# A block kernel on one core: five sums of squares and sums, from fp32 operands to split fp32r ones

## The reference, cut to what matters

```python
def rms_norm(x, g):
    y = x * rsqrt(mean(x * x, -1) + EPS)
    return y * g
...
# gated linear attention, 4 heads of 128: a norm over the 128 features of each head
o = o * rsqrt(mean(o * o, -1) + EPS)
...
# conformer_conv, 512 channels: a depthwise convolution of width 31, then a layer norm over the channels
y = conv(a * sigmoid(g)) + dw_b
mu = mean(y, -1)
xc = y - mu
y = silu(xc * rsqrt(mean(xc * xc, -1) + EPS) * ln_g + ln_b)
...
# the norm ahead of the feed forward part
hn = rms_norm(h, norm2_g)
h = h + square(relu(hn @ w_ff1)) @ w_ff2
```

## Time and profile before

| what | us |
|---|---|
| median of 3 runs | 878.4 (877.93 to 878.43) |
| the profiled execution | 878.33 |
| its span | 877.0 |
| TensorE busy with matmuls | 867.4 |
| VectorE busy | 725.4 |
| ScalarE busy | 573.4 |

### The profile page before, as it was taken

The page is one execution under the profiler, slowest core; times in us unless marked ns, Lnnn a source line. Parts: engine busy times, 40 slices in busy tenths (PEclk is TensorE's granted clock), DMA queues, the critical chain, the costliest instruction groups (busy, mean ns, idle before and its releaser), DMA issues.

```text
span 877.0 us, 18438 instructions
## 1 busy us (share of the span) xinstructions
PE 867.4 (99%) x7308; PEld 846.6 (97%) x7308; DVE 725.4 (83%) x1168; ACT 573.4 (65%) x851; POOL 2.2 (0%) x10
## 2 busy tenths in 40 slices
PE   9999999999999999999999999999999999999996
PEld 7999989999999999999999999899999999999996
DVE  6788999899988899888887999989788985555554
ACT  7858466675696787664446879677786664444542
POOL 0000000000000000000000000000000000000000
PEclk9999999999999999999999999999999999999999
DMA  8866456566775789989895566754455566666551
GB/s 316 284 197 225 149 164 194 170 191 211 271 243 191 257 290 332 324 299 339 328 336 180 168 220 209 209 166 141 152 166 176 187 201 200 192 194 195 182 161 49
DMA packets 59045, 189.87 MB, mean 216 GB/s; under 512 B 8640, under 2 KB 11088, under 8 KB 58832
## 3 DMA queue, kind: packets, MB, share of 16 engines
q1 hardware_dynamic: 58816, 188.69, 65.0%
q10 hardware_dynamic: 144, 0.00, 0.0%
HBM read 186.57 MB, written 1.05 MB: 214 GB/s over the span
## 4 chain that ended last, share of the span: by engine, by line
PE 91%; ACT 4%; DVE 3%; issue 1%; DMA 1%; SPq 0%; DVEq 0%; ACTq 0%
PE bank L1101 28%; PE bank L1103 27%; PE bank L1104 27%; PE bank L1074 1%; PE bank L1073 1%; PE bank L1072 1%; ACT whi L2048 1%; DMA H<-in_xT 1%; PE bank L1035 0%; DVE wlo L1146 0%; PE bank L1042 0%; PE bank L1038 0%; PE bank L887 0%; PE bank L769 0%; ACT L2252 0%
## 5 line engine op out<-in xcount | busy, mean ns | idle before, releaser
L1146 DVE TENSOR_TENSOR wlo<-raw,whi 128x1024 fp32r<-128x1024 f32 x291 | 353.7, 1221 | 83.2 <-ACT whi L2048 82.6
L2048 ACT ACTIVATE whi<-raw 128x1024 fp32r<-128x1024 f32 x291 | 304.7, 1056 | 169.0 <-PE bank L1104 164.2
L1101 PE MATMUL bank<-Alo,whi 128*128 128x256 f32 x1328 | 371.5, 280 | 0.0
L1103 PE MATMUL bank<-Ahi,wlo 128*128 128x256 f32 x1328 | 367.7, 277 | 0.0
L1104 PE MATMUL bank<-Ahi,whi 128*128 128x256 f32 x1328 | 367.7, 277 | 0.0
L1101 PEld LDWEIGHTS bank<-Alo,whi 128*128 128x128 f32 x1328 | 249.9, 188 | 2.8 <-issue 2.2
L1103 PEld LDWEIGHTS bank<-Ahi,wlo 128*128 128x128 f32 x1328 | 249.5, 188 | 0.4 <-issue 0.2
L1104 PEld LDWEIGHTS bank<-Ahi,whi 128*128 128x128 f32 x1328 | 249.5, 188 | 0.0
L1103 PE MATMUL bank<-Fhi,wlo 128*128 128x256 f32 (+1 forms) x320 | 88.9, 278 | 0.0
L1104 PE MATMUL bank<-Fhi,whi 128*128 128x256 f32 (+1 forms) x320 | 88.9, 278 | 0.0
L1101 PE MATMUL bank<-Flo,whi 128*128 128x256 f32 x256 | 70.8, 277 | 0.0
(11 more groups left out here) (447 smaller groups left out, 1378.3 us busy)
## 6 DMA issues: line engine op xcount, KB each, us to landing
raw<-in_stream SPq DMA_DIRECT2D x298, 512.0 KB, 4.3
arows<-in_ada SPq DMA_DIRECT2D x64, 384.0 KB, 5.2
TB<-in_TB SPq DMA_DIRECT2D x1, 1536.0 KB, 7.2
a8r<-a SPq DMA_DIRECT2D x16, 64.0 KB, 4.2
out<-H SPq DMA_DIRECT2D x4, 256.0 KB, 2.9
bc<-in_bc SPq DMA_DIRECT2D x1, 896.0 KB, 5.7
H<-in_xT SPq DMA_DIRECT2D x1, 512.0 KB, 7.2
mats<-in_mats SPq DMA_DIRECT2D x1, 449.0 KB, 7.2
```

Of the source, the lines that this page charges most:

```text
L1101: pe.matmul(os[j], wh, xl, start=k == 0 and (wide or j == 0), stop=False, skip_group_check=not wide)
L1103: pe.matmul(os[j], wl, xh, start=False, stop=False, skip_group_check=not wide)
L1146: v.tensor_tensor(wlo[:, s % NHL, :], raw[:, s % NRAW, :], whi[:, s % NHL, :].bitcast(F32), ALU.subtract).then_inc(*lo_v.up(s))
L2048: a.activation(whi[:, s % NHL, :], raw[:, s % NRAW, :], ACT.Copy).then_inc(*hi.up(s))
```

## The change

The five sums get split operands. ScalarE copies the values to fp32r (the high part), VectorE subtracts to get the low part, and `streamed` sends both through `onesr` as two fp32r matmuls into one sum. For the gated attention the parts lie in the slots of heads 1 and 3 in `Yhi[2]` and `Ylo[2]`, which are written with their own values later; for the convolution in a new tile `sumc`, over the memory of `P1`, so that the first copy waits for the attention to be done; for `r2` in a new tile `sum2`. `onesr` is set to ones by GpSimd at the start, and no longer copied by ScalarE in the second block. The table `STEPS` gets steps for the copies and subtractions. For `gla` TensorE's sums move from 34 and 39 to 35 and 40; VectorE has the subtractions at 35 and 40, and what followed moves from 36, 38, 41, 43 to 37, 39, 42, 44; ScalarE moves from 34, 37, 39, 42 to 35, 38, 40, 43. For `conv` the sums stay at 73 and 78.5, the copies are at ScalarE's 72 and 77, the subtractions at VectorE's 73 and 78. `r2` moves from 98 to 99, with the copy at 97, the subtraction at 98.

```diff
@@ -192,17 +192,17 @@
     "sg": ([15, 15], [9, 12, 13, 16, 17, 22, 24, 25, 26], [10, 23, 24]),
-    "gla": ([19, 26, 28, 32, 34, 39], [20, 22, 24, 27, 29, 30, 36, 38, 41, 43],
-            [20, 21, 22, 26, 33, 34, 37, 39, 42]),
+    "gla": ([19, 26, 28, 32, 35, 40], [20, 22, 24, 27, 29, 30, 35, 37, 39, 40, 42, 44],
+            [20, 21, 22, 26, 33, 35, 38, 40, 43]),
     "att": ([44, 49, 50.5, 50.5, 55, 56, 56, 61, 62.5, 62.5, 67, 68],
...
             [n for h in range(4) for n in (45 + 6 * h, 49 + 6 * h, 50 + 6 * h)]),
-    "conv": ([73, 78.5], [*(n for n in range(18, 70) if n not in (36, 41, 63, 64)), 72, 75, 76, 79, 80, 81, 82, 83],
-             [73, 75, 78, 79, 80, 81, 82]),
+    "conv": ([73, 78.5], [*(n for n in range(18, 70) if n not in (36, 41, 63, 64)), 72, 73, 75, 76, 78, 79, 80, 81, 82, 83],
+             [72, 73, 75, 77, 78, 79, 80, 81, 82]),
     "trig": ([], [98, 100, 102, 104, 106, 108], [104, 110]),
...
     "sums": ([SUMS], [SUMS + 1, SUMS + 2], []),
-    "r2": ([98], [96, 100, 101], [98]),
+    "r2": ([99], [96, 98, 101, 102], [97, 99]),
     "xb": ([], [173, 174, 175, 176, 177, 177], [174, 175, 176, 177]),
@@ -311,6 +311,7 @@
         ones = sb("ones", [128, 128])
+        onesr = sb("onesr", [128, 128], F32R)
         cosT = sb("cosT", [128, T])
@@ -366,6 +367,9 @@
         scr = s1("scr", [128, 1024])
+        p1s = ExitStack()
+        sumc = sb("sumc", [128, 2, T], F32R, p1s)
+        p1s.close()
         P1 = s1("P1", [128, 2, 384])
@@ -386,6 +390,7 @@
         ftmp = s2("ftmp", [128, 512])
+        sum2 = s2("sum2", [128, 2, T], F32R)
         p2.close()
@@ -403,8 +408,7 @@
         bgates = s3("bgates", [128, 8])
-        onesr = s3("onesr", [128, 128], F32R)
-        s3("gap3", [128, 8])
+        s3("gap3", [128, 136])
         bc2 = s3("bc2", [128, 512])
@@ -482,7 +486,7 @@
         sq, added, summed, root, rstd = signals("sq added summed root rstd")
-        ones_v, pad_g, sgm_g, tbm_g, mpad_g = signals("ones_v pad_g sgm_g tbm_g mpad_g")
+        ones_v, ones_g, pad_g, sgm_g, tbm_g, mpad_g = signals("ones_v ones_g pad_g sgm_g tbm_g mpad_g")
@@ -651,6 +655,11 @@
+            def streamed(b, high, low):
+                w.wait_ge(*ones_g.at("set"))
+                pe.matmul(b, onesr[:, :], high, start=True, stop=False)
+                return pe.matmul(b, onesr[:, :], low, start=False, stop=True)
+
             def r1():
@@ -664,10 +673,9 @@
                 w.wait_ge(*att_v.at("lo", 3))
-                for n, tag in enumerate(("mean", "var")):
-                    w.wait_ge(*conv_v.at("sum", tag))
-                    pe.matmul(banks[3][:, 0:T], ones[:, :], scr[:, n * 512:n * 512 + T], start=True, stop=True
-                              ).then_inc(*conv_pe.up(tag))
+                for tag in ("mean", "var"):
+                    w.wait_ge(*conv_v.at("rest", tag))
+                    streamed(banks[3][:, 0:T], sumc[:, 0, :], sumc[:, 1, :]).then_inc(*conv_pe.up(tag))
                     yield
@@ -739,9 +747,8 @@
                         w.wait_ge(*gla_s.at("root", 0))
-                    w.wait_ge(*gla_s.at("sq", hf))
-                    pe.matmul(banks[7][:, :], ones[:, :], scr[:, 0:512], start=True, stop=True
-                              ).then_inc(*gla_pe.up("n", hf))
+                    w.wait_ge(*gla_v.at("rest", hf))
+                    streamed(banks[7][:, :], Yhi[2][:, 1::2, :], Ylo[2][:, 1::2, :]).then_inc(*gla_pe.up("n", hf))
                     yield
@@ -793,7 +800,8 @@
             def r2():
-                total("r2", 3)
+                w.wait_ge(*added.at("r2", 4))
+                streamed(banks[3][:, 0:T], sum2[:, 0, :], sum2[:, 1, :]).then_inc(*summed.up("r2"))
                 yield
@@ -862,9 +870,7 @@
                         w.wait_ge(*ml_v.at("nlo", hp, i))
-                        pe.matmul(banks[3 + i][:, 0:T], onesr[:, :], nhi[:, i, :], start=True, stop=False)
-                        pe.matmul(banks[3 + i][:, 0:T], onesr[:, :], nlo[:, i, :], start=False, stop=True
-                                  ).then_inc(*ml_pe.up("n", hp, i))
+                        streamed(banks[3 + i][:, 0:T], nhi[:, i, :], nlo[:, i, :]).then_inc(*ml_pe.up("n", hp, i))
                     yield
@@ -1230,6 +1236,11 @@
+            def rest(tag, n):
+                w.wait_ge(*conv_s.at("high", tag))
+                v.tensor_tensor(sumc[:, 1, :], scr[:, n * 512:n * 512 + T], sumc[:, 0, :].bitcast(F32), ALU.subtract
+                                ).then_inc(*conv_v.up("rest", tag))
+
             def conv():
@@ -1252,6 +1263,8 @@
                 yield
+                rest("mean", 0)
+                yield
                 w.wait_ge(*conv_s.at("mu"))
@@ -1261,6 +1274,8 @@
                 added_up("var", scr[:, 512:512 + T], scr[:, 512 + T:1024])
+                yield
+                rest("var", 1)
                 yield
@@ -1355,6 +1370,12 @@
                     b, s, o = banks[(6, 5)[hf]], scr[:, 0:512], scr[:, 512:1024]
+                    w.wait_ge(*gla_s.at("high", hf))
+                    if hf:
+                        w.wait_ge(*gla_pe.at("n", 0))
+                    v.tensor_tensor(Ylo[2][:, 1::2, :], s.rearrange("p (a t) -> p a t", a=2),
+                                    Yhi[2][:, 1::2, :].bitcast(F32), ALU.subtract).then_inc(*gla_v.up("rest", hf))
+                    yield
                     w.wait_ge(*gla_s.at("root", hf))
@@ -1501,6 +1522,9 @@
                 v.tensor_scalar(g2, g2, EPS, None, ALU.add).then_inc(*mod_v.up("g2"))
+                yield
+                w.wait_ge(*sq.at("r2", 4))
+                v.tensor_tensor(sum2[:, 1, :], acc, sum2[:, 0, :].bitcast(F32), ALU.subtract).then_inc(*added.up("r2", 4))
                 yield
@@ -2087,12 +2111,23 @@
+            def high(tag, n):
+                w.wait_ge(*conv_v.at("sum", tag))
+                if n:
+                    w.wait_ge(*conv_pe.at("mean"))
+                a.activation(sumc[:, 0, :], scr[:, n * 512:n * 512 + T], ACT.Copy).then_inc(*conv_s.up("high", tag))
+
             def conv():
+                w.wait_ge(*att_pe.at("o", 3, 1))
+                high("mean", 0)
+                yield
                 w.wait_ge(*conv_pe.at("mean"))
...
                 a.activation(ypad[:, :, 0:T], cv[:, :, :], ACT.Square).then_inc(*conv_s.up("sq"))
+                yield
+                high("var", 1)
                 yield
@@ -2140,6 +2175,9 @@
                     a.activation(scr[:, 0:512], banks[(6, 5)[hf]][:, :], ACT.Square).then_inc(*gla_s.up("sq", hf))
+                    w.wait_ge(*gla_s.at("sq", hf))
+                    a.activation(Yhi[2][:, 1::2, :], scr[:, 0:512].rearrange("p (a t) -> p a t", a=2), ACT.Copy
+                                 ).then_inc(*gla_s.up("high", hf))
                     yield
@@ -2209,6 +2247,9 @@
             def r2():
+                w.wait_ge(*added.at("r2", 3))
+                a.activation(sum2[:, 0, :], acc, ACT.Copy).then_inc(*sq.up("r2", 4))
+                yield
                 square_root("r2", 3)
@@ -2260,7 +2301,6 @@
                 a.activation(lf[:, :, :], lf[:, :, :], ACT.Ln, bias=1.0).then_inc(*ifg_s.up("ln"))
-                a.activation(onesr[:, :], ones[:, :], ACT.Copy).then_inc(*ifg_s.up("ones"))
                 yield
@@ -2577,6 +2617,7 @@
             w = Waiting(g)
+            g.memset(onesr[:, :].bitcast(F32), 1.0).then_inc(*ones_g.up("set"))
             g.memset(ypad[:, :, 0:30], 0.0).then_inc(*pad_g.up("set"))
...
             w.wait_ge(*sgw_in.at("in"))
```

## The result

The changed kernel takes 896.6 us (median of four executions: 893.3, 895.3, 897.9 and 901.8) against 878.4 (four, 877.9 to 879.7): 1.021 times the time before, with a 95% interval of 1.016 to 1.026. I had forecast 888.9. The direction was right, and so was the place of every wait; the size of the loss was not: 18 us, not 10.5.

The account below looks back on a forecast made before the run. TensorE, busy 867.4 of 877.0 us, was taken as the bound, so waits add to the end. Five waits of 11.9 us less 1.45 saved gave +10.5 us on 878.4, forecast 888.9 us, 8 in 10 range 885.0 to 893.5.

Parts of the forecast that it names:

- The count of steps against slabs: At all five sums, when VectorE's subtraction is done against when TensorE arrives; waits of 11.9 us in all.
- The first two waits: At the gated attention's two norms, TensorE waits 3.15 and 4.01 us for subtractions, net +2.74 and +3.60.
- the detour of the second through `whi` of slab 40: Before the second attention norm, VectorE idles for `whi` of slab 40, which comes 2.74 us later.
- The mean: At the convolution's mean, after slab 73, TensorE waits 2.4 us for the subtraction, net +2.2.
- Variance and `r2`: At the convolution's variance and at `r2`, waits of 1.22 and 1.11 us, net +1.0 and +0.9.
- the saving of 1.45 us: At all five sums, two fp32r matmuls replace one fp32 matmul: 0.82 us saved for attention, 0.63 for the others.
- rival (a): TensorE's clock falls in one or both long attention waits: 890.5 to 894 us, chance 0.28.
- My price: From the opening `ones` matmuls, 421 ns against 275: one fall of the clock costs up to 2.5 us.
- My argument against it: The clock fell at the end after TensorE was only partly busy; each wait here stands between dense slabs.
- (b): The second attention norm costs less as VectorE has caught up: 885 to 887 us, chance 0.12.
- (d): Only the first wait or two stay, the rest is absorbed by waiting work: 880.5 to 884 us, chance 0.08.
- (c): At all five sums the subtractions are done when TensorE arrives, only 1.45 saved stays: 877.0 us, chance 0.04.

Follow-up runs that it names:

- warm: The changed kernel with 13, 17 and 9 small matmuls filling the waits before both attention norms and the mean: 888.2 to 891.6 and 897.4 to 898.1 us.
- waits_fp32: The changed kernel with all its copies, subtractions, steps and waits, but fp32 sums of the unsplit values: 893.6 to 905.1 us.
- conv_only: Only the convolution's mean and variance changed against the kernel before: 882.4, 882.7 and 889.2 to 891.2 us.
- conv_third: The kernel with only the convolution's mean and variance changed, run a third time for a trace; this and the second run gave 881.2 and 891.4 us.
- wait_fp32: Only the convolution's copies, subtractions and waits added to the kernel before, but TensorE sums the unsplit values in fp32: 882.3 to 885.9 us.
- after_plain: The changed kernel with two more small fp32 matmuls, after slabs 76 and 81: 894.2 to 902.6 us.
- conv_again: The kernel with only the convolution's mean and variance changed, run a second time for a trace; this and the third run gave 881.2 and 891.4 us.
- conv_plain: Only the convolution's mean and variance changed, plus two small fp32 matmuls after slabs 76 and 81: 881.8 to 883.6 and 889.5 to 890.3 us.
- the retimed versions: The changed kernel's split sums with subtractions earlier or sums later, to avoid the waits; the first such version took 876.9 to 877.7 and 879.7 to 880.0 us.
- r2_early: Only `r2` changed against the kernel before, its subtraction at step 97 instead of 98, so without a wait: ten at 877.0 to 879.2 us, one 884.8.
- the last version: The first version without waits, with one `ada` product moved behind the variance's subtraction and one more tap moved: ten at 876.6 to 877.9 us, one 882.9.

## Why the prediction was right and wrong

**The waits, right.** The count of steps against slabs, on which all rested, holds in five places out of five. The first two waits came within about 0.1 us (3.16 and 4.12 for 3.15 and 4.01), with the detour of the second through `whi` of slab 40. The mean came at 2.42 for 2.4. Variance and `r2` were 0.5 and 0.3 shorter than forecast, because TensorE, at its slower pace, came later itself: in the trace of warm, with the pace at 0.113 ahead of both, they are 1.23 and 1.11 by starts. That the loss comes with the waits is shown from both sides: with the waits and without the pairs it is no smaller, and with the pairs and without the waits it is gone (876.6 to 877.9 us in ten of eleven executions; forecast for that case: 877.0). Of the saving of 1.45 us the medians there show 1.0.

**The clock, wrong.** The step that failed is "I keep it as a rival". The sum was made at full clock, so this term stood at nothing, and rival (a), with a chance of 0.28, counted one or two falls at 2.5 us. There were three, at 1.7 us each, 5.1 in all. My price came from the opening matmuls on `ones`, which were no rows of a fall: the profile grants 1.00 there, from 0 to 6 us. And the price is not one number, since two falls of waits_fp32 took 3.4 each. My argument against it, that each wait stands between dense slabs, is refuted by rows: even the mean's wait of 2.4 us was enough, in six of the eight traces that have it without filling (the changed kernel, conv_only, conv_third, wait_fp32, after_plain and waits_fp32; not in conv_again and conv_plain). The Trainium skill, "TensorE: Matmul & The Clock Gate", Part 1, has the rule that idleness brings the half rate back and activity lifts it; the traces agree in the main, with 0.50 granted behind each of the three waits (119 to 121, 139 to 142 and 245 to 247 us of the changed kernel's trace), though behind the same wait of 2.4 us it fell in some executions only. With two falls at my price the forecast would have been 893.9, with the three that came, at 1.7, 894.0.

**The pace, not thought of.** No row that I read showed that the distance between matmuls can be 0.118 instead of 0.113 for hundreds of microseconds. The trace of before has it, from 93 to 104 us for instance, but I took 0.113 from one place and used it as a constant. This second step failed too: a term that the sum doesn't have was 2.7 us in the profiled execution, and the traces of a short and a long execution of conv_only differ by it. How much of the changed kernel's spread from 893.3 to 901.8 it makes is not shown, beside the clock.

**The rivals.** (a) came true in its mechanism and was too small, since it counted on two falls at most and no slower pace. (b), a second norm that costs less, and (d), absorption, are refuted by the 4.12 us and by slab 100. (c), no waits, is what the retimed versions did.

What stays open is why the pace sometimes changes where the stream of matmuls is broken, why a fall of the clock costs 1.7 us in most traces and 3.4 in two places of one, why wait_fp32 showed no long execution in five, and what made the one long execution each of r2_early and of the last version.

## What to carry to other kernels

Where one engine is the bound and its queue is in order, a matmul that is made cheaper by a few tenths must not wait for a new helper: write down when the helper's result is done and when the bound engine arrives, both from the trace, and place the consumer a step behind. Bubbles of two to four microseconds on TensorE cost here one and a half times to nearly twice their length (9.7 us of them, and behind them 5.1 of clock and 2.7 of pace in the profiled execution), so they should be priced with these and not at their length. And a change whose gain is a tenth of a per cent needs some ten executions, on one chip, and a look at their groups, since a median of a few falls in one group or the other by chance.

## What the runs showed of the hardware that was not expected

- TensorE has two paces at a granted clock of 1.00: matmuls of 256 columns 0.113 us apart, or 0.118 (442 to 444 against 425 to 427 in 50 us). The changes seen stand where the stream of alike matmuls is broken (a wait, a gap of 0.28 us, small fp32 matmuls, once a pair on `onesr` that had not to wait), though not every such place changes it, and then the pace holds, in one trace for 243 us. For comparison the Trainium skill, "TensorE: Matmul & The Clock Gate", Part 1, gives columns at 2.4 GHz and about 2.5 ns a matmul, by which I estimate 109 ns for 256 columns; neither pace is that.
- With a wait of about 1 us ahead of one sum, 10 of 24 executions were 6 to 7 us longer than the others, and one more 13 us; the one long execution that was traced has the slower pace for 170 us behind it (304.2 to 474.6 us). Of the kernel before, which has no such wait, no execution was longer than 881.1 us.
- The clock fell behind a wait of 2.4 us in one execution of a kernel and not in another of the same kernel (0.50 and 1.00 granted from 234 to 236 us). A fall cost 1.7 us in most traces, and 3.4 in two of the three falls of waits_fp32.
